# Interleaving the second request group's attention with its convolution

## What is computed

```
h = rms_norm(x) * (1 + scale1) + shift1
q, k, v, B, C, X, g_att, g_conv = split(h @ w_in)         # q, k, v: 8 heads x 64; B, C, X: 512 channels
q, k = rms_norm(q) * q_gain, rms_norm(k) * k_gain
y_att = softmax(q k^T / 8 + bias) v @ w_o_att             # banded, chunks of 64
y_conv = (B * conv3(C * X)) @ w_o_conv                    # causal, 3 taps a channel
x += gate1 * (sigmoid(g_att) * y_att + sigmoid(g_conv) * y_conv) @ w_o
h2 = rms_norm(x) * (1 + scale2) + shift2
for each frame and each of 8 heads:                       # product-key retrieval
    top 16 of 128 + 128 sub-key scores -> 16 experts of 16384
    x += gate2 * sum(softmax(score) * gelu(u[expert] . h2) * v[expert])
```

## Time and profile before

| | us |
|---|---|
| median of 3 runs | 2029.66 |
| the profiled execution | 2043.05 |
| its span in the profile | 2041.0 |
| TensorE busy | 1634.1 (80%) |
| VectorE busy | 1205.5 (59%) |
| ScalarE busy | 721.4 (35%) |
| POOL busy | 628.5 (31%) |

### The profile page before, as it was taken

How to read it: one execution, slowest core, us unless ns; L and a number is a source line. 1 busy time by engine, 2 the same in 40 slices (tenths; PEclk the granted TensorE clock), 3 DMA queues, 4 the chain that set the end, 5 groups by cost and what they waited for, 6 DMA issues and landing times.

```text
span 2041.0 us, 22251 instructions
## 1 busy us (share of the span) xinstructions
PE 1634.1 (80%) x7437; PEld 784.4 (38%) x7437; DVE 1205.5 (59%) x3104; ACT 721.4 (35%) x2231; POOL 628.5 (31%) x584
## 2 busy tenths in 40 slices
PE   6999998977887789889889677676676776767776
PEld 4775786844443345445355321121121121211221
DVE  2425112787787675544677667777766666665554
ACT  2215201353266543322423243333333333333332
POOL 0000000143331343333333254444343444343431
PEclk8999999998977799999999999998998999999989
DMA  9557520699995799999998699999999999999996
GB/s 399 205 189 269 194 91 21 247 375 362 395 366 220 291 411 421 421 421 411 414 389 322 253 423 421 421 422 421 422 421 421 421 422 421 422 420 422 422 420 249
DMA packets 100386, 718.22 MB, mean 352 GB/s; under 512 B 11488, under 2 KB 11504, under 8 KB 13488
## 3 DMA queue, kind: packets, MB, share of 16 engines
q0 software_dynamic: 82944, 604.02, 72.2%
q1 hardware_dynamic: 16464, 110.43, 13.9%
q10 hardware_dynamic: 864, 2.36, 0.3%
HBM read 712.04 MB, written 4.73 MB: 351 GB/s over the span
## 4 chain that ended last, share of the span: by engine, by line
DMA 42%; PE 29%; DVE 14%; issue 8%; ACT 4%; POOL 3%; SPq 0%; another core or an unknown queue 0%; DVEq 0%; POOLq 0%; ACTq 0%
DMA ring<-in_expert_uv_dram,uidx 41%; PE ps L877 7%; PE ps L612 6%; DVE ring L1544 6%; PE ps L736 4%; POOL ring L480 3%; PE ps L757 3%; PE ps L742 2%; DMA ring<-in_wpack_dram 1%; PE ps L608 1%; ACT wsel L1134 1%; PE ps L642 1%; PE ps L857 1%; ACT wdiag L1139 1%; DVE left L1447 1%
## 5 line engine op out<-in xcount | busy, mean ns | idle before, releaser
L877 PE MATMUL ps<-ring,wdiag 128*32 128x512 f32 x2304 | 814.1, 673 | 282.4 <-ACT wdiag L1139 206.6
L480 POOL DMA_INDIRECT ring<-in_expert_uv_dram,uidx x576 | 627.2, 1089 | 1328.8 <-PE ps L877 853.3
L1544 DVE CUSTOM_DVE_ANT_0 ring<-ring,mA 128x1024 f32<-128x1024 f32 x576 | 699.4, 1223 | 472.7 <-DMA ring<-in_expert_uv_dram,uidx 456.6
L877 PEld LDWEIGHTS ps<-ring,wdiag 128*32 128x32 f32 x2304 | 170.6, 118 | 846.1 <-ACT wdiag L1139 455.2
L1132 ACT ACTIVATE gel<-act_in 128x1 f32<-128x1 f32 x576 | 116.6, 202 | 854.7 <-DVE act_in L1544 839.8
L1139 ACT ACTIVATE wdiag<-repeat,wsel 128x32 f32<-128x32 f32 x576 | 185.1, 321 | 18.8
L1134 ACT ACTIVATE wsel<-gel,gsel 128x1 f32<-128x1 f32 x576 | 169.7, 295 | 18.7
L612 PE MATMUL ps<-hB,ring 128*128 128x320 f32 x320 | 93.1, 440 | 0.7 <-ACT convB L991 0.7
L612 PE MATMUL ps<-hA,ring 128*128 128x256 f32 x320 | 73.5, 391 | 6.8 <-DVE qB L1264 3.7
L795 PE MATMUL ps<-hB,ring 128*128 128x320 f32 x256 | 77.2, 455 | 0.0
L736 PE MATMUL ps<-hB,ring 128*128 128x320 f32 x256 | 73.2, 439 | 0.0
(11 more groups left out here) (241 smaller groups left out, 1593.7 us busy)
## 6 DMA issues: line engine op xcount, KB each, us to landing
ring<-in_wpack_dram SPq DMA_DIRECT2D x96, 1024.0 KB, 5.8
ring<-in_expert_uv_dram,uidx POOLq DMA_INDIRECT x576
xB<-in_x_b_dram SPq DMA_DIRECT2D x2, 1280.0 KB, 19.3
o_y_p<-mA ACTq DMA_DIRECT2D x16, 128.0 KB
xA<-in_x_a_dram SPq DMA_DIRECT2D x1, 1024.0 KB, 5.2
bias<-in_bias_dram SPq DMA_DIRECT2D x1, 1024.0 KB, 32.0
o_v_p<-kv SPq DMA_DIRECT2D x4, 256.0 KB, 13.4
o_k_p<-xB SPq DMA_DIRECT2D x4, 256.0 KB, 7.5
```

Of the source, the lines that this page charges most:

```text
L480: nc.gpsimd.indirect_dma_start(out=ring[:, slot, :], out_offset=None, in_=ins["expert_uv"], in_offset=bass.IndirectOffsetOnAxis(ap=uidx[:, ...
L877: mm = nc.tensor.matmul(pY[c * GT:(c + 1) * GT, half, :], wdiag[:, n % NDIAG, :], ring[:, ROW[n][0], D + half * 512:D + (half + 1) * 512], ...
L1544: nc.vector.tensor_tensor_reduce(r, r, h2n[:, g % 2, :], 1.0, 0.0, ALU.mult, ALU.add, act_in[:, g % 2, j:j + 1]).then_inc(s["dot"], 1)
```

## The change

In `ticks(1)`, only the first 30 half-results of `z` (results 0 to 14) stand ahead of the attention; the other 22 stand one behind each of the attention steps 0 to 21. Their number and pace in `ORDER` stay. The banks follow: all group 1 results from 11 on use bank 3 alone, and all its scores use bank 2 alone. The waits are changed to suit: the first scores wait for group 0's key scores to be copied and no longer for the whole of `z`; every score waits for the read of the score before; the first V product waits for the v copies; the state turn and the merge wait for the last convolution result.

```diff
--- before.py
+++ after.py
@@ -82,6 +82,9 @@
 
 
 LAG = 3
+WITH_A = 3 + 2 * (8 + len(TOKENS[1]))
+BEHIND = WITH_A // 2 - 1
+AMONG = BEHIND + PH // 2
 
 
 def ticks(g):
@@ -94,10 +97,13 @@
     if g == 0:
         out += [("ada", 0, t) for t in range(KD // 2, KD)]
     out.append(("norm", 0, 2))
-    out += [("z", r, piece) for r in range(len(ZR[g])) for piece in range(2)]
+    pieces = [("z", r, piece) for r in range(len(ZR[g])) for piece in range(2)]
+    ahead = 2 * AMONG if g else len(pieces)
+    out += pieces[:ahead]
     nu = len(units(g))
     for u in range(nu + LAG + 2):
         out.append(("at", u, 0))
+        out += pieces[ahead + u:ahead + u + 1]
         if g == 0 and u < 2 * KD:
             out.append(("ada", 1 + u // KD, u % KD))
     out += [("kn", i, 0) for i in range(len(TOKENS[g]))]
@@ -129,9 +135,6 @@
     return hd + 1 if p == 0 else PH + p
 
 
-WITH_A = 3 + 2 * (8 + len(TOKENS[1]))
-BEHIND = WITH_A // 2 - 1
-AMONG = BEHIND + PH // 2
 
 
 NORM_AT = [("z", 6, 1), ("z", 9, 1), ("z", 11, 1)]
@@ -432,7 +435,10 @@
         PO = (6, 1)
 
         def zbank(g, r):
-            return BK[1][1] if g == 1 and BEHIND <= r < AMONG else BK[g][r % 2]
+            return BK[1][1] if g == 1 and r >= BEHIND else BK[g][r % 2]
+
+        def sbank(g, u):
+            return BK[1][0] if g == 1 else BK[0][u % 2]
 
         def zbefore(g, r):
             same = [x for x in range(r) if zbank(g, x) == zbank(g, r)]
@@ -592,8 +598,6 @@
                             pe.wait_ge(s[f"h_act{g}"], KD // 2 * len(SEGS[g]))
                             pe.wait_ge(s[f"h_dve{g}"], KD // 2 * len(SEGS[g]))
                             pe.wait_ge(s[f"mean{g}"], 1)
-                        if g == 1 and r == AMONG:
-                            pe.wait_ge(s["sc_sb0"], len(TOKENS[0]) * PH)
                         b4 = zbefore(g, r)
                         if b4 is not None:
                             if ZR[g][b4][0] == "qk":
@@ -625,12 +629,17 @@
                     h0 = (hd % 2) * HD
                     if u == 0:
                         pe.wait_ge(s[f"zqk{g}"], 8)
-                        pe.wait_ge(s[f"zd{g}"], ZD[g][-1])
-                        pe.wait_ge(s[f"za{g}"], ZA[g][-1])
+                        if g == 0:
+                            pe.wait_ge(s["zd0"], ZD[0][-1])
+                            pe.wait_ge(s["za0"], ZA[0][-1])
+                        else:
+                            pe.wait_ge(s["sc_sb0"], len(TOKENS[0]) * PH)
                     if g == 1 and i == 2 and hd == 0:
                         pe.wait_ge(s["k_cache"], 16)
-                    if u >= 2:
-                        pe.wait_ge(s[f"s_dve{g}"], u - 1)
+                    if g == 0 and u >= 2:
+                        pe.wait_ge(s["s_dve0"], u - 1)
+                    if g == 1 and u:
+                        pe.wait_ge(s["s_dve1"], u)
                     q = qT[g][h0:h0 + HD, hd // 2, c0:c0 + w]
                     at = 0
                     parts = key_parts(g, i)
@@ -639,7 +648,7 @@
                         while kind == "new" and parts and parts[0][0] == "new" and parts[0][1] == k0 + kw:
                             kw += parts.pop(0)[2]
                         keys = kcT[h0:h0 + HD, hd // 2, :] if kind == "past" else kT[h0:h0 + HD, hd // 2, k0:k0 + kw]
-                        mm = nc.tensor.matmul(ps[0:w, BK[g][u % 2], at:at + kw], q, keys, start=True, stop=True)
+                        mm = nc.tensor.matmul(ps[0:w, sbank(g, u), at:at + kw], q, keys, start=True, stop=True)
                         at += kw
                     mm.then_inc(s[f"s_ps{g}"], 1)
 
@@ -665,6 +674,8 @@
                     i, hd = units(g)[u]
                     w = TOKENS[g][i][1]
                     pe.wait_ge(s[f"pt{g}"], u + 1)
+                    if g == 1 and u == 0:
+                        pe.wait_ge(s["za1"], ZA[1][8 + 2 * len(TOKENS[1])])
                     if g == 1 and i == 2 and hd == 0:
                         pe.wait_ge(s["v_cache"], 16)
                     if hd == 0 and i:
@@ -711,6 +722,7 @@
 
                 def conv_state():
                     pe.wait_ge(s["kn1"], len(TOKENS[1]))
+                    pe.wait_ge(s["zd1"], ZD[1][-1])
                     nc.tensor.transpose(ps[0:16, PT[1][0], 0:P], cst[:, :, :, :].rearrange("p g w c -> p (g w c)"),
                                         ident[:, :]).then_inc(s["state_ps"], 1)
 
@@ -720,6 +732,7 @@
                     bank = BK[g][res % 2]
                     if q == 0 and d == 0:
                         pe.wait_ge(s[f"s_dve{g}"], len(units(g)))
+                        pe.wait_ge(s[f"zd{g}"], ZD[g][-1])
                     if q == 0 and d:
                         pe.wait_ge(s[f"mdve{g}"], 2 * d - 1)
                     if q == 2 and d:
@@ -1326,7 +1339,7 @@
                     if nk == P + TS:
                         b = b[:, 0:P + TS]
                     first = max(nk - 256, 0)
-                    src, dst = ps[0:w, BK[g][u % 2], :], att_sc[0:w, u % 3, :]
+                    src, dst = ps[0:w, sbank(g, u), :], att_sc[0:w, u % 3, :]
                     if first:
                         cd.did(nc.vector.tensor_scalar(dst[:, 0:first], src[:, 0:first], HD ** -0.5, b[:, 0:1],
                                                        ALU.mult, ALU.add))
```

## The result

The changed kernel took 2036.03 us (median of 14), the kernel before 2029.83 us beside it: ratio 1.0036, 95% interval 1.0024 to 1.0049. A second comparison, later and with its own runs of before, gave 1.0000 (0.9987 to 1.0013). So the change does nothing or costs up to 0.5%. The forecast was 28 us faster.

The account below looks back on a forecast made before the run. It took expert-row loads, starved by a chain of TensorE, ScalarE and VectorE waits in rows 28 to 97, as the bound. 32.4 - 4.4 = 28.0 us off 2029.66 gave 2001.7 us; 8-in-10 range 1981 to 2028.

Parts of the forecast that it names:

- The step that failed: Group 1's units 0 to 21 with half-results: 169.6 us at VectorE 0.905 busy, 32.4 us less than 202.
- my sum: Rows 28 to 97: 32.4 us won less 4.4 for late tile copies, 28.0 us saved.
- the finished tile: Units 11, 19 and drain: TensorE still waits for ScalarE's copy; 4.4 us lost, bounds 0 and 8.8.
- VectorE as the bound: Units 0 to 21: VectorE's 153.5 us of work at 0.905 busy sets the pace, above traffic and TensorE.
- VectorE keeps today's share: Rival, rows 28 to 97: VectorE stays 0.75 busy, nothing won, 2024 to 2034 us; chance 0.16.
- One bank each: Group 1's scores and convolution results wait for single banks: 0 us over units 0 to 21; convolution bounds 0 and 14.
- the sign of lock-step: Idle before the convolution's first matmul, put down to VectorE, or before the scores, beyond 10 us together.
- The lock-step rival: Convolution steps too wait for another engine: 65 us idle, stretch 261 us, 16 more, 2046 us; chance 0.10.
- the traffic ceiling: Rows 28 to 97 at 421 GB/s need 193.2 us, so at most 51.8 us can be won.
- TensorE under its limit: Per pair of steps in units 0 to 21, TensorE needs 6.7 us against the DMA's 7.05.
- the moved waits: First scores, first values, state turn and merge wait for other, earlier signals: all 0 us.
- the clock: Rival: half-results also run at clock 0.76, so 22 of the 28 us go, 2024 us; chance 0.04.

Follow-up runs that it names:

- the other mends: Changed kernel plus finished tile's copy ahead of the exponentials, convolution bank freed behind the multiplication, store three rows later: 2022.82 us (0.9921); with exponentials one row later too, 2014.91 us (0.9893).
- with a quarter of its work gone: Changed kernel without VectorE's top-k picks for the second tile of group 0: 2019.92 us, 0.9952 of the kernel before.
- the table loads: Exp in place of gelu for the 576 rows' weights, sparing ScalarE's table loads: 2024.28 us (0.9978) on the changed kernel, 2023.92 us (0.9984) on the kernel before.
- The fastest kernel but one: Changed kernel with only group 1's exponentials one row later in ScalarE's queue, behind the next row's weights: 2018.43 us, 0.9902 of the kernel before.

## Why the prediction was wrong

**The step that failed** is "so units 0 to 21 with their half-results should take 153.5 / 0.905 = 169.6 us". They took 205 (481 to 686), with the same 153.5 us of VectorE's work that 482 to 684 held before in 202. I read the chain of three engines rightly, but took its price for one of space: with 2.58 rows between units, I thought, each link would have time. The chain that holds the rows does not run from step to step. It lies within one: at every second step ScalarE needs the maximum of the unit whose scores TensorE issues in that same step, behind whatever VectorE has queued. Space between steps takes nothing off it (23.2 us before, 24.3 after), and the weights of rows that have landed wait behind it. Moved one row back in ScalarE's queue, the wait is gone and the stretch takes 211.6 us with the other mends and 216.9 with this edit alone. Counted alike, my sum had about 211; that 211.6 meets it is partly luck, since it takes mends that the sum did not have. So the gain was there to be had, but not by the change that I forecast it for. I had seen this for the finished tile ("no half-result comes between") and not for the exponentials, 12 pairs against two or three tiles.

**VectorE as the bound** was the wrong measure. 0.905 came from one stretch of 43 us, and in the windows of after VectorE is never more than 0.81 busy. The rival "VectorE keeps today's share" gave the right number (0.75; unchanged time). As a limit of VectorE the runs don't bear it out: with a quarter of its work gone the rate rose to 361 GB/s only. What its queue does is make the maxima late.

**The finished tile**, a term I took at 4.4 us within 0 to 8.8: its waits grew to 13.1 us. It is the same mechanism: the copy stands behind the pair of exponentials, and these behind the maximum. At unit 11 the scores were issued at 582.83, and VectorE, with two dot products and a pick ahead of them, scaled them at 588.32, 5.5 us later; before it was 2.3 us (628.58 to 630.87). Moving the copy brought 12.3 us. The upper bound from the row of before was not one.

**One bank each**, taken at 0, within 0 to 14 us for the convolution: 6 us in the old order, where the waits sum to 27. In the new order they sum to 9.3 us, just under the 10 that I had named as the sign of lock-step; what they cost there was not measured by itself. The lock-step rival (2046) had the mechanism in part, and too dear.

**Right:** the traffic ceiling, which no run passed; TensorE under its limit; 0 for SP, POOL and the moved waits (TensorE waits for no weight block and for none of the moved signals in the view); the clock, which didn't fall over the whole (0.86, was 0.84) and rose to 0.92 when the stretch filled. The rule weighed there is from the Trainium skill, "TensorE: Matmul & The Clock Gate", Part 4: PE-mode transpose: transposes do not count as busy for the clock as other matmuls do. By it they could have pulled the convolution's clock down. The half-results ran at a granted clock of 0.92 beside units 0 to 9, against 0.96 by themselves before, so whatever the transposes did to it cost little here. That nothing is given back behind row 97 held too.

**Open:** how much of the changed kernel's 0 to 0.36% is the banks, and how much the store below; and whether the table loads bring more interleaved. The medians say twice as much (11.8 to 5.3 us), but across groups of runs, and the profile of that kernel is also one of those without the held store.

## What to carry to other kernels

Before spacing out a chain of engines to hide it, see whether its links lie between steps or within one: here the ones within a step gained nothing from space. Where an engine walks one fixed order, ask what stands behind each of its waits; here one row's shift of 24 exponentials in ScalarE's queue, behind work that was ready and behind the tile's copy, came to 20 us under before where the large move alone brought nothing, and it needed that move to do so. A wait read before a change is no upper bound for it afterwards: what it waits for can come later.

## What the hardware showed

ScalarE's issue of one 128 KB store takes 0.32 to 0.38 us in this kernel. The first of them in the interleaved order held its queue for 5.59 us:

```profile
561.34 5.59 ACTq L1169 DMA_DIRECT2D o_y_p<-mA  x1
```

Of the twelve profiles in the interleaved order, eight show 4.0 to 5.6 us there, among them both of the changed kernel; the other four, three of them with the store later, show 0.38, and so do all eight in the old order. No view names what it waited for. The DMA moved 370 GB/s while it was held (561 to 567 us); around the same store of before, which took 0.38 us, it moved 421 and 423. One thing goes with it in the record: in all eight, SP issued a 1.05 MB weight block 2.5 to 4.8 us behind the store's start; in eleven of the other twelve that block had been issued 5 us or more ahead of the store. In the twelfth it was issued 1.5 us behind, and the store took 0.38 us. Since the block comes after the hold has begun, this shows no cause, and none was found. The fastest kernel but one has the hold (4.82 us) and still takes 0.9902.
